# The value pages of the sample's first four batches, moved ahead of the prompt's retention chunks

## The reference

```python
x = LN1(alpha*x + 0.5*SwiGLU_1(x))
x = LN2(alpha*x + Mix(x))
x = LN3(alpha*x + 0.5*SwiGLU_2(x))
```

```python
inner = einsum('bnhd,bmhd->bhnm', q, k) * decay
intra = einsum('bhnm,bmhe->bnhe', inner, v)
cross = einsum('bnhd,bhde->bnhe', q, s_prev) * xi
s_new = exp(L*lg) * s_prev + einsum('bmhd,bmhe->bhde', k * zeta, v)
```

## Time and profile before

| | |
|---|---|
| runs | 1650.62 to 1655.94 us, median 1653.21 |
| profiled execution | 1664.57 us, of which the span of the trace is 1662.9 |
| busy, of the span | PE 95%, PEld 81%, DVE 43%, ACT 26%, POOL 8% |
| TensorE's granted clock | 0.95 of full on the mean |
| the chain that ended last | PE 86%, DVE 4%, ACT 3%, SP's queue 2%, transfers 2%, issue 2% |

### The profile page before, as it was taken

The page is one execution under the profiler, slowest core; times in us unless marked ns, Lnnn a source line. Parts: engine busy times, 40 slices in busy tenths (PEclk is TensorE's granted clock), DMA queues, the critical chain, the costliest instruction groups (busy, mean ns, idle before and its releaser), DMA issues.

```text
span 1662.9 us, 27542 instructions
## 1 busy us (share of the span) xinstructions
PE 1578.0 (95%) x10137; PEld 1353.2 (81%) x10137; DVE 714.2 (43%) x1138; ACT 432.9 (26%) x697; POOL 127.4 (8%) x186
## 2 busy tenths in 40 slices
PE   7999999999999999999987798998989999999995
PEld 6999999999764689989764354445779999999995
DVE  3323323222414688888475435661152332332224
ACT  3433432212323200000211002440063333332123
POOL 0000000332130000000020010000140000000001
PEclk9999999999999999999998956889989999999998
DMA  4222222332132455554406732542212222222231
GB/s 183 89 79 85 88 83 78 94 115 86 55 101 63 131 182 179 173 175 150 162 13 178 220 114 91 157 140 79 73 37 78 88 88 77 87 85 71 82 91 55
DMA packets 73219, 176.88 MB, mean 106 GB/s; under 512 B 9681, under 2 KB 13778, under 8 KB 72914
## 3 DMA queue, kind: packets, MB, share of 16 engines
q1 hardware_dynamic: 67730, 164.20, 31.7%
q0 software_dynamic: 4576, 8.13, 1.5%
q10 hardware_dynamic: 864, 3.91, 0.6%
HBM read 169.11 MB, written 7.09 MB: 106 GB/s over the span
## 4 chain that ended last, share of the span: by engine, by line
PE 86%; DVE 4%; ACT 3%; SPq 2%; DMA 2%; issue 2%; POOL 0%; ACTq 0%; DVEq 0%; PEldq 0%
PE ps L312 85%; PE ps L315 2%; SPq L198 1%; SPq L254 1%; ACT scr L730 1%; ACT xbuf L730 1%; DMA xbuf<-in_x_t 1%; DVE rbuf L1012 1%; DMA out_rs_o<-dring 1%; DVE scr L1021 1%; ACT x_high L730 0%; DVE mxb L1136 0%; DVE big L1012 0%; DVE w_low L951 0%; DVE lg L1150 0%
## 5 line engine op out<-in xcount | busy, mean ns | idle before, releaser
L312 PE MATMUL ps<-x_high,w_high 128*128 128x280 f32 x1408 | 417.7, 297 | 16.5 <-DVE x_low L957 10.6
L312 PE MATMUL ps<-x_high,w_low 128*128 128x280 f32 x1408 | 415.9, 295 | 0.0
L312 PE MATMUL ps<-x_low,w_high 128*128 128x280 f32 x1408 | 414.2, 294 | 0.0
L951 DVE TENSOR_TENSOR w_low<-wring,w_high 128x1024 fp32r<-128x1024 f32 (+1 forms) x136 | 162.8, 1198 | 519.8 <-ACT w_high L730 519.7
L312 PEld LDWEIGHTS ps<-x_high,w_high 128*128 128x128 f32 x1408 | 269.0, 191 | 21.6 <-issue 13.0
L312 PEld LDWEIGHTS ps<-x_low,w_high 128*128 128x128 f32 x1408 | 269.4, 191 | 0.0
L312 PEld LDWEIGHTS ps<-x_high,w_low 128*128 128x128 f32 x1408 | 268.0, 190 | 0.0
L730 ACT ACTIVATE w_high<-wring 128x1024 fp32r<-128x1024 f32 (+1 forms) x136 | 140.6, 1035 | 434.3 <-PE ps L312 429.3
L312 PE MATMUL ps<-xbuf,wring 128*128 128x280 f32 x928 | 239.3, 409 | 1.2 <-DVE sc L1078 0.9
L312 PEld LDWEIGHTS ps<-xbuf,wring 128*128 128x128 f32 x928 | 172.3, 192 | 42.2 <-issue 4.2
L312 PE MATMUL ps<-h_low,w_high 128*128 128x280 f32 x704 | 205.4, 292 | 0.0
(11 more groups left out here) (155 smaller groups left out, 1428.7 us busy)
## 6 DMA issues: line engine op xcount, KB each, us to landing
dring<-in_k_pool SPq DMA_DIRECT2D x128, 256.0 KB, 2.8
dring<-in_v_pool SPq DMA_DIRECT2D x128, 256.0 KB, 2.9
wring<-in_wg SPq DMA_DIRECT2D x44, 512.0 KB, 3.5
wring<-in_wu SPq DMA_DIRECT2D x44, 512.0 KB, 3.5
wring<-in_wd SPq DMA_DIRECT2D x32, 512.0 KB, 3.6
wring<-in_w_in SPq DMA_DIRECT2D x29, 512.0 KB, 3.7
wring<-in_wd SPq DMA_DIRECT2D x16, 384.0 KB, 3.1
wring<-in_w_out SPq DMA_DIRECT2D x8, 512.0 KB, 3.7
```

The source lines that it names most:

```text
L312: return nc.tensor.matmul(out, lhs, rhs, start=start, stop=stop, **kw)
L951: v.tensor_tensor(wl[:, to, 0:n], w4[:, s, 0:n], wh[:, to, 0:n].bitcast(F32), ALU.subtract) \
```

## The change

`value_pages` is called once, for all 64 pages of batches 0 to 3, ahead of the loop over the chunks. The calls inside the chunks and behind the sample's `ret_in` go, and `FILL` with them. On ACT the copy of bank 5 moves from between the last two square roots to ahead of the loop.

```diff
-FILL = [4, 4, 4]
...
+            value_pages(NPAGE * 4)
             for cn in range(5):
                 t0, n = (128 * cn, P) if cn < 4 else (TL, TAIL)
                 vv = vr[:, cn, :] if cn < 4 else vrt
                 ret_in(cn, t0, n)
-                value_pages(FILL[0])
                 pe.wait_ge(sem("it_done"), cn + 1)
...
                 last.then_inc(sem("rst_full"), 1)
-                value_pages(min(FILL[1], NPAGE * 4 - done[0]))
                 ret_out(cn, n)
-                value_pages(min(FILL[2], NPAGE * 4 - done[0]))
                 pe.wait_ge(sem("mixr_done"), cn + 1)
             ret_in(5, SMP, NS)
-            value_pages(NPAGE * 4 - done[0])
             pe.wait_ge(sem("so_out"), 1)
...
             gate(3, 3)
+            act.wait_ge(sem("so_full"), 1)
+            ev(lg[:, 0:512], ps[:, 5, :]).then_inc(sem("so_out"), 1)
             for cn in range(6):
...
-                if cn == 4:
-                    act.wait_ge(sem("so_full"), 1)
-                    ev(lg[:, 0:512], ps[:, 5, :]).then_inc(sem("so_out"), 1)
```

## The result

The kernel after takes 1720.27 us (median of 4 runs, 1717.64 to 1724.88), the kernel before 1651.91 (4 runs: the three known to the prediction, with a median of 1653.21, and one of 1646.03). The ratio is 1.0409, 95% interval 1.0375 to 1.0443: slower by 68 us, and 0.3 us from the predicted 1720. Two terms behind that number were off, in opposite directions, as the rest shows.

A forecast was written before the change was run, and what follows sets the result against it. It took SP's issue pace of 1.24 us a page as the bound, hiding the chunks. Pages to 970.0, chunks 68.7 and step 3.45 put the first state's product 67.5 us later: 1720 us from 1653.2, range 1696 to 1731.

The forecast's parts named there:

- What bounds the kernel: Stretch from 878 to 1010 us: SP's issue at 1.24 us a page sets the end; the retention chunks run beneath it.
- The pages alone, 970.0: Page phase ahead of the chunks: ends at 970.0 us with the last eight matmuls at half clock, 962.6 at full clock.
- The chunks, 68.7: Five retention chunks with no pages beside them: 68.7 us, between 55.0 at full clock and 73.3 at half clock.
- full-clock sum of 55.0: Five uncovered chunks at full clock: three full ones 34.9 us, chunk 0 9.8, chunk 4 10.3, together 55.0.
- three quarters of the way: Clock guess for the chunks: 55.0 + 0.75 x 18.3 = 68.7 us, toward the half-clock bound of 73.3.
- The step to the sample, 3.45: From the chunks' end to the first state's product: sample's first matmuls 1.54 plus four matmuls 1.91, 3.45 us.
- The sum, 67.5: First state's product at 970.0 + 68.7 + 3.45 = 1042.2 us instead of 974.70, 67.5 us later.
- Carried over to the median: Whole kernel: 67.5 us added to 1653.2, as the profiled execution stood 11.4 us above the median, giving 1720 us.
- full clock throughout: Rival: pages and chunks all at full clock, product 44.6 us later, 1698 us; chance 0.11.
- slow pages with fast chunks: Rival: pages end at 970.0, chunks take 55.0 at full clock, product 53.7 us later, 1707 us; chance 0.13.
- Pages one after another: Rival: half-clock pages don't overlap on PE, 64 take 122.9 us, product 111 us later, 1764 us; chance 0.05.
- a faster stream of SP's: Rival, not slower: PE's late releases pace SP, whose page stream then speeds up, 1653 us or below; chance 0.03.

The follow-up runs named there:

- second trace of before: The unchanged kernel before, run and traced once more: 1652.31 us.
- the idle matmuls: The change plus idle matmuls into an unused bank in PE's gaps of each chunk: 1709.28 us, ratio 1.0328 to the kernel before.
- the run with the copy back: The change on PE alone, with ACT's copy of bank 5 left between the last two square roots as before: 1722.63 us, one run.
- half of the pages ahead: The kernel before with 32 pages ahead of the chunks, 28 between their steps, 4 behind the sample's first step: 1688.82 us, ratio 1.0188.
- two queues: The kernel before with POOL issuing every second of the first 64 pages: 1648.76 us; also with 4, 8, 0 pages a chunk: 1643.39 us.
- 4, 8, 0 on one queue: The kernel before with FILL 4, 8, 0 instead of 4, 4, 4 pages between a chunk's steps, SP's queue alone: 1653.60 us, ratio 0.9997.

## Why the prediction was right, and where it was not

*What bounds the kernel*: right. SP's pace is 1.22 us after and 1.24 before; a second queue shortens the stream, a new order on one queue does not.

*The pages alone, 970.0*: mis-sized, measured 961.92. The stream itself came as summed; the eight last matmuls were taken at 0.50 from 955.2 and ran at 1.00, 955.11 to 961.99 for the partners and the pages among them. The full-clock bound of that term was 962.6. The prediction had turned against the Trainium skill (TensorE: Matmul & The Clock Gate, "What's actually happening") on the strength of the 14.8 us at 0.50. For this phase the Trainium skill's rule, that activity releases the slow clock, was the better guide, and the trace agrees with it: the first burst of pages, 882.79 to 889.87, was dense, the clock was 1.00 from 890 on, and the lone pages held it there, PE busy 3.6 to 5.0 of 5 us. Behind the stretch the same trace does not agree, as the last section shows. In the trace before the clock had fallen in the gap of the last chunk, and these matmuls didn't bring it back; in the second trace of before it had fallen too, and they did. So the 14.8 us were one outcome of two, and the prediction took them for a property of narrow matmuls.

*The chunks, 68.7*: right, measured 69.4. The full-clock sum of 55.0 was measured as 56.5 by the idle matmuls, and "three quarters of the way" to 73.3 was close to the distances of 14.9, 15.6 and 15.0 us of the three full chunks. Of the sum's parts only chunk 0, at 10.7 us, was near its full-clock end, since it still had the pages' clock.

*The step to the sample, 3.45*: measured 1034.71 - 1031.34 = 3.37.

*The sum, 67.5*: 60.0 in the traces: -8.1 from the pages, +0.7 from the chunks. With the pages' full-clock bound in the pages' place the prediction's own numbers give it: 962.6 + 68.7 + 3.45 = 1034.75, measured 1034.71. This mix, pages at full clock and chunks mostly at half, was not among its cases; carried over in its way it would have given 1653.2 + 60.05 = 1713 us, 7 below what was measured.

*Carried over to the median*: the step that failed unseen. The prediction subtracted the 11.4 us by which the traced execution stood above the median as if it were the same in both kernels. It was not: the traced execution of the change, at 1724.88, stands 4.6 above its median. Of the 11.4, 7.3 us are the clock in this very stretch, which the other trace of before doesn't have, while the two traces with the change's order on PE (the change and the run with the copy back) agree from first page to product, 151.9 and 152.4 us. That the 1720 was met to 0.3 us comes from these two errors, -8 and +8, cancelling. The mechanism is shown; the last digits are luck.

*The rivals*: full clock throughout is half right (pages yes, chunks no), and slow pages with fast chunks is the reverse of what came. Pages one after another and a faster stream of SP's did not happen.

## What to carry to other kernels

Where two jobs lie side by side, find which one sets the end and what paces it: here a queue's issue, 1.24 us a page, with a 55 to 69 us chain hidden beneath it. Taking them apart in either order costs the whole of the hidden one, and the clock that is lost in its gaps on top; neither order on the waiting engine changes the pace of the queue. Before a traced execution is used as the base of a sum, compare its own time with the median, and ask in which stretch the difference sits, since a stretch that the change rebuilds does not carry it over.

## What the runs showed of the hardware that was not expected

The same eight matmuls of pages and partners ran at 0.50 for 14.8 us in one execution of the kernel before, and in 8.5 us in another, where the clock rose to 1.00 during the first of them. It had been at 0.50 ahead of them in both, so what it was when they began does not decide it. The other traces that have these eight in this place fall to both sides: 14.8 us with half of the pages ahead, 8.9 and 8.6 with two queues, 7.9 with 4, 8, 0 on one queue. Why the clock rose in some and not in others stays open. Lone page matmuls with a wait between them, PE busy 4.38 of 5 us, ran at 1.00 once it was there, for 70 us. In the same trace of the change a PE just as busy, 30.67 of 35 us, ran at 0.50 throughout on the sample's state matmuls behind the stretch:

```profile
1035.00:1070.00 35.00, 30.67 (x128) 23.92 (x126) 16.82 (x41) 1.48 (x2) 7.22 (x13) 0.50 0.32 98
```

And with two queues that issue pages at once the transfers reached 304 GB/s on the mean, where the change with one queue had 213 in the same 50 us, though each landing then took a median of 4.4 us (SP's) and 4.5 (POOL's) instead of 3.0.
